# Convolution, norms and first queries of a streaming encoder step placed differently in the engines' queues

## What is computed

```python
def token_mixers(xn, hist_a, hist_b, w_in, ...):
    proj = xn @ w_in                                   # 2560 columns: h_a, c_a, b_a, v_b, g_b, 512 each
    conv_out_a, new_a = causal_dwconv(hist_a, c_a * h_a, conv_a_w)        # 3 taps
    y_a = rmsnorm(b_a * conv_out_a, out_norm_a_g)
    glu = v_b * sigmoid(g_b)
    conv_out_b, new_b = causal_dwconv(hist_b, glu, conv_b_w)              # 31 taps
    z = silu(layernorm(conv_out_b + conv_b_b, conv_norm_g, conv_norm_b))
    y_b = rmsnorm(z, out_norm_b_g)
    return concatenate([y_a, y_b]) @ w_out, new_a, new_b

h = x + token_mixers(rmsnorm(x), ...)
q = rmsnorm(h) @ w_q                                   # 2048 columns: 16 queries a token
x = h + peer(q, ...)                                   # top-k keys, 16384 single-neuron experts
y = rmsnorm(x)
```

## Time and profile before

| | us |
|---|---|
| median of 3 runs (1466.56 to 1467.59) | 1467.55 |
| the profiled execution | 1467.65 |
| span of its instructions | 1465.9 |
| before the first or behind the last of them | 1.75 |
| PE busy | 1448.5 (99%) |
| DVE busy | 1231.5 (84%) |
| POOL busy | 878.5 (60%) |
| ACT busy | 628.1 (43%) |
| mean granted TensorE clock | 0.995 |

### The profile page before, as it was taken

How to read it: one execution, slowest core, us unless ns; L and a number is a source line. 1 busy time by engine, 2 the same in 40 slices (tenths; PEclk the granted TensorE clock), 3 DMA queues, 4 the chain that set the end, 5 groups by cost and what they waited for, 6 DMA issues and landing times.

```text
span 1465.9 us, 25025 instructions
## 1 busy us (share of the span) xinstructions
PE 1448.5 (99%) x8592; PEld 1323.2 (90%) x8592; DVE 1231.5 (84%) x2517; ACT 628.1 (43%) x845; POOL 878.5 (60%) x551
## 2 busy tenths in 40 slices
PE   9998989999999999999999999999999999999998
PEld 9998989999999999999999999888888888888886
DVE  6998876898999999488788851799999999999995
ACT  6334543333333333467666754333333333333333
POOL 5686534556888888667666775255555555555510
PEclk9999999999999999999999999999999999999999
DMA  5321223567999999779999999899999999999962
GB/s 195 101 86 57 91 73 118 199 215 241 317 341 347 340 348 339 254 285 370 365 365 359 373 364 379 319 370 387 381 400 384 403 384 393 371 407 378 384 249 90
DMA packets 120259, 433.35 MB, mean 296 GB/s; under 512 B 12384, under 2 KB 12640, under 8 KB 118528
## 3 DMA queue, kind: packets, MB, share of 16 engines
q1 hardware_dynamic: 62592, 212.88, 40.3%
q0 software_dynamic: 46080, 167.79, 30.2%
q10 hardware_dynamic: 11520, 51.93, 8.9%
HBM read 379.34 MB, written 52.69 MB: 295 GB/s over the span
## 4 chain that ended last, share of the span: by engine, by line
PE 84%; DVE 1%; issue 0%; ACT 0%; DVEq 0%; ACTq 0%
PE ps_unit L861 36%; PE ps_misc L930 24%; PE ps_unit L930 12%; PE ps_unit L834 6%; PE ps_misc L896 3%; PE ps_misc L799 1%; PE ps_misc L803 0%; PE ps_unit L786 0%; PE ps_misc L926 0%; DVE gate L1577 0%; DVE gate_parts L1622 0%; PE ps_unit L926 0%; PE ps_misc L915 0%; PE ps_misc L817 0%; PE ps_misc L878 0%
## 5 line engine op out<-in xcount | busy, mean ns | idle before, releaser
L515 POOL TENSOR_TENSOR w_lo<-raw,w_hi 128x1024 fp32r<-128x1024 f32 x171 | 413.0, 2416 | 200.5 <-issue 120.9
L579 POOL DMA_INDIRECT rows<-v_rows,expert x160 | 256.7, 1604 | 243.0 <-DVE sums L1489 163.3
L976 ACT ACTIVATE w_hi<-raw 128x1024 fp32r<-128x1024 f32 x300 | 315.3, 1051 | 49.1 <-ACT act_ring L1152 31.8
L1196 ACT ACTIVATE prod_hi<-prod 128x384 fp32r<-128x384 f32 x128 | 67.3, 526 | 329.7 <-PE ps_unit L930 329.0
L861 PE MATMUL ps_unit<-mov_hi,w_hi 128*128 128x384 f32 x1024 | 204.6, 341 | 0.0
L861 PE MATMUL ps_unit<-mov_hi,w_lo 128*128 128x384 f32 x1024 | 199.9, 337 | 0.0
L861 PE MATMUL ps_unit<-mov_lo,w_hi 128*128 128x384 f32 x1024 | 199.9, 337 | 0.0
L1479 DVE CUSTOM_DVE_ANT_0 rows<-rows,ps_unit 128x1024 f32<-128x1024 f32 x160 | 189.5, 1213 | 5.5 <-DMA rows<-u_rows,expert 5.5
L861 PEld LDWEIGHTS ps_unit<-mov_lo,w_hi 128*128 128x128 f32 x1024 | 180.9, 188 | 0.0
L861 PEld LDWEIGHTS ps_unit<-mov_hi,w_lo 128*128 128x128 f32 x1024 | 180.9, 188 | 0.0
L861 PEld LDWEIGHTS ps_unit<-mov_hi,w_hi 128*128 128x128 f32 x1024 | 178.1, 188 | 0.2 <-issue 0.2
(11 more groups left out here) (263 smaller groups left out, 2563.0 us busy)
## 6 DMA issues: line engine op xcount, KB each, us to landing
raw<-stream SPq DMA_DIRECT2D x300, 512.0 KB, 6.1
acts_dram<-act_ring ACTq DMA_DIRECT2D x64, 384.0 KB
gates_dram<-gates ACTq DMA_DIRECT2D x12, 2048.0 KB, 10.9
acts_in<-acts_dram SPq DMA_DIRECT2D x32, 768.0 KB, 8.7
gates_even<-gates_dram SPq DMA_DIRECT2D x12, 1024.0 KB, 12.9
gates_odd<-gates_dram SPq DMA_DIRECT2D x12, 1024.0 KB, 13.2
rows<-u_rows,expert POOLq DMA_INDIRECT x160, 6.7
rows<-v_rows,expert POOLq DMA_INDIRECT x160, 8.4
```

The source lines that it names most:

```text
L515: nc.gpsimd.tensor_tensor(w_lo[:, j, :], raw[:, j, :], w_hi[:, j, :].bitcast(F32), ALU.subtract).then_inc(lo_made, 1)
L579: nc.gpsimd.indirect_dma_start(out=rows[:, n % ROWS_RING, :], out_offset=None, in_=table, in_offset=bass.IndirectOffsetOnAxis(ap=expert[:, ...
L976: nc.scalar.activation(w_hi[:, j, :], raw[:, j, :], ACT.Copy).then_inc(hi_made, 1)
L1196: nc.scalar.activation(prod_hi[:, v % RING], prod[:, v % 2], ACT.Copy).then_inc(prod_hi_made, 1)
```

## The change

The convolution's products: POOL makes `pad_b` for chunks 1 to 3 in its loop over units, at units 5, 7 and 9, ahead of that unit's wait for ACT. Chunk 0's stay on DVE, with the scaling of unit 1 that POOL had, and POOL waits for them. The sum of channels runs inside unit 19, between its second and third chunk. Of unit 20, the passes that need only `mov_hi` run as its chunks come, and the passes with `mov_lo` after the sum for the narrow norm. On DVE the last chunk's narrow taps are added before the `mov_low` steps, `reciprocal(2)` stands before the last of these, `reciprocal(3)` and the first two `add_output` come before the scaling of the layernorm, and the copies to the cache come after it. On ACT, the squares of the centred chunks precede the take of unit 19, the root's table is loaded at unit 8, and the squares of the narrow part follow `root(3)`. PE takes unit 23 before the sum for the second group's norm, runs 12 matmuls of ones by ones (`BUSY_FFN`) ahead of the queries, and takes the two first queries side by side, in the second half with a lag of three chunks. In unit 1, PE takes the second part of the first norm's sum of squares at k = 3 in place of 6. The diff's parts stand in the order POOL, PE, ACT, DVE.

```diff
                     split_low(0, 3)
                     pool.wait_ge(rstd_made, 1)
+                    pool.wait_ge(first_pad_made, 1)
...
+                if u in (5, 7, 9):
+                    n = (u - 3) // 2
+                    pool.wait_ge(sigmoid_made, n + 1)
+                    pool.wait_ge(in_scaled, 2 * n)
+                    pool.wait_ge(pads_ready, 1)
+                    times(pad_b[:, n, HIST_B:HIST_B + T_PROMPT], proj[:, 2 * n, 0:T_PROMPT],
+                          proj[:, 2 * n + 1, 0:T_PROMPT])
+                    times(pad_b[:, n, 2 * HIST_B + T_PROMPT:PAD_B], ...).then_inc(pad_b_made, 1)
...
+                    if c == WC - 1:
+                        step(times(b, b, rstd[:]))
+                        pool.wait_ge(taps_added, 1)
+                        times(h, h, b).then_inc(ya_made, 1)
+                        continue
...
                 for k in range(KC):
                     if k == 1:
                         square_sum(sq[:, KC - 1], sq_made, KC, False)
-                    if k == KC - 2:
+                    if k == 3:
                         square_sum(sq[:, 0], sq_added, 1, True)
...
-            with pe.Fori(1, N_IN // RING) as lap:
+            with pe.Fori(1, N_IN // RING - 1) as lap:
...
+            def sum_conv():
+                pe.wait_ge(conv_b_made, WC)
+                channel_sum(lambda c: proj[:, 2 * c], range(WC), WC, 0)
+
+            for j in range(RING):
+                pe.wait_ge(act_took, N_IN - RING + j - 1)
+                unit(N_IN // RING - 1, j, mov_hi, mov_lo, sum_conv if j == RING - 1 else None)
...
             channel_sum(lambda c: sq[:, c], range(WC), WC, 1, SQ_X + WC - 1)
+            pe.wait_ge(act_took, N_IN)
+            pe.wait_ge(hi_made, FIRST_OUT + 1)
+            pe.wait_ge(lo_made, FIRST_OUT + 1)
+            for k in range(WC):
+                pe.wait_ge(mov_hi_made, KC + k + 1)
+                for o in range(2):
+                    first_out(o, w_hi, mov_hi, k, first=(k == 0))
+                    first_out(o, w_lo, mov_hi, k)
             pe.wait_ge(a_added, 1)
             pe.wait_ge(sq_made, SQ_X + 2 * WC)
             channel_sum(lambda n: sq[:, (WC, KC - 1)[n]], range(2), 2, 0)
-            pe.wait_ge(act_took, N_IN)
-            out_unit(0, 0)
+            for o in range(2):
+                for k in range(WC):
+                    pe.wait_ge(mov_lo_made, KC + k + 1)
+                    ins = first_out(o, w_hi, mov_lo, k, last=(k == WC - 1))
+                ins.then_inc(unit_done if o else out_half_done, 1)
             out_unit(0, 1)
             out_unit(0, 2)
+            out_unit(0, 3)
             pe.wait_ge(dve_took, WC)
             pe.wait_ge(silu_added, 1)
             channel_sum(lambda c: sq[:, c], (0,), 1, 1)
-            out_unit(0, 3)
...
+                for a, lag in ((0, 0), (1, 3)):
+                    for k in range(KC + lag):
+                        for j, kj in ((0, k), (1, k - lag)):
+                            if not 0 <= kj < KC:
+                                continue
...
+            keep_busy(ps_unit[:, 0, 0:P], BUSY_FFN)
             first_queries()
...
+                if u == N_IN - 1:
+                    for n in range(WC):
+                        act.wait_ge(centred, n + 1)
+                        nc.scalar.activation(sq[:, n], proj[:, 2 * n], ACT.Square).then_inc(sq_made, 1)
                 if u > 0:
                     take(0, u, proj[:, u])
...
+            root(3, 1, 1.0 / WIDTH)
             act.wait_ge(ya_made, WC)
             group_high(WC - 1, ...)
             squares_a(WC - 1)
-            root(3, 1, 1.0 / WIDTH)
+            root(4, 0, 1.0 / WIDTH, out=std_a)
             split_high(first_out, 2)
             split_high(first_out, 3)
-            act.wait_ge(rstd_made, 2)
-            root(4, 0, 1.0 / WIDTH)
             act.wait_ge(cache_made, 1)
             act.dma_start(caches, cache_out[:]).then_inc(cache_saved, 16)
             for c in range(WC):
                 act.wait_ge(scaled_b, c + 1)
...
+            dve.wait_ge(sum_done, 2)
+            for c in range(WC):
+                nc.vector.scalar_tensor_tensor(out=halves(proj[:, 2 * c]), ...).then_inc(centred, 1)
+            dve.wait_ge(taps_made, WC)
...
+            nc.vector.tensor_tensor(h[:, 0:T_PROMPT], taps[0][:, 0:T_PROMPT], taps[2][:, 0:T_PROMPT],
+                                    ALU.add).then_inc(taps_added, 1)
+            for c in range(WC - 1):
+                mov_low(KC + c, c, proj[:, 2 * WC + 3 * c], par_col("out_a_g", c))
+            reciprocal(2, rstd_c)
             mov_low(KC + WC - 1, WC - 1, ...)
...
-            reciprocal(2, rstd[:])
-            dve.wait_ge(rstd_made, 2)
+            reciprocal(3, rstd_a, std_a)
+            dve.wait_ge(rstd_made, 3)
+            for q in range(2):
+                add_output(q, rstd_a)
             dve.wait_ge(centred, WC)
             for c in range(WC):
-                nc.vector.tensor_tensor(proj[:, 2 * c], proj[:, 2 * c], rstd[:], ALU.mult).then_inc(scaled_b, 1)
-            reciprocal(3, rstd_a)
-            dve.wait_ge(rstd_made, 3)
-            for q in range(KC - 2):
+                nc.vector.tensor_tensor(proj[:, 2 * c], proj[:, 2 * c], rstd_c, ALU.mult).then_inc(scaled_b, 1)
...
+            last.then_inc(cache_made, 1)
+            for q in range(2, KC - 2):
                 add_output(q, rstd_a)
             for c in range(WC):
                 mov_low(KC + WC + c, WC + c, proj[:, 2 * c + 1], par_col("out_b_g", c))
             for q in range(KC - 2, KC):
                 add_output(q, rstd_a)
```

More of the change, by code:

```diff
@@ L99 @@
 MADE_AHEAD = AHEAD + 1
+BUSY_FFN = 12
 WARM_UP = 12
@@ L285, in build @@
         a_added = sem("a_added")
+        taps_added = sem("taps_added")
         silu_added = sem("silu_added")
@@ L619, in _, with unit @@
         def _(pe):
-            def unit(lap, j, hi, lo):
+            def unit(lap, j, hi, lo, between=None):
                 u = RING * lap + j
@@ L626, in unit @@
                 for k in range(KC):
+                    if between and k == 2:
+                        between()
                     for n, (w, m) in enumerate(((w_hi, hi), (w_hi, lo), (w_lo, hi))):
@@ L632, in unit, with keep_busy @@
                 last.then_inc(unit_done, 1)
+            def keep_busy(out, times):
+                for n in range(times):
+                    nc.tensor.matmul(out, ones[:], ones[:], start=True, stop=True)
             def channel_sum(src, ks, chunks, to, n_sq=None):
@@ L734, in out_unit, with first_out @@
                     last.then_inc(unit_done if o else out_half_done, 1)
-            pe.wait_ge(conv_b_made, WC)
-            channel_sum(lambda c: proj[:, 2 * c], range(WC), WC, 0)
-            channel_sum(lambda c: sq[:, c], range(WC), WC, 1, SQ_X + WC - 1)
+            def first_out(o, w, mov, k, first=False, last=False):
+                at = (WC * o + k) * P
+                for a in range(2):
+                    ins = nc.tensor.matmul(out_psum(o)[:, a, :], w[:, 0, at:at + P], half(mov[:, k], a),
+                                           start=first, stop=last)
+                return ins
+            channel_sum(lambda c: sq[:, c], range(WC), WC, 1, SQ_X + WC - 1)
+            pe.wait_ge(act_took, N_IN)
[6 more added lines that the diff above has]
+                    first_out(o, w_lo, mov_hi, k)
             pe.wait_ge(a_added, 1)
@@ L771, in first_queries @@
             def first_queries():
[L773 to L778, removed]
+                for j in range(2):
+                    pe.wait_ge(hi_made, FIRST_Q + j + 1)
+                    pe.wait_ge(lo_made, FIRST_Q + j + 1)
+                for a, lag in ((0, 0), (1, 3)):
[3 more added lines that the diff above has]
+                                continue
                             if j == 0:
@@ L785, in first_queries @@
                             for m, (w, mov) in enumerate(((w_hi, mov_hi), (w_hi, mov_lo), (w_lo, mov_hi))):
[L786 to L790, removed]
+                                last = nc.tensor.matmul(unit_psum(j)[:, a, :], w[:, j, kj * P:(kj + 1) * P],
+                                                        half(mov[:, kj], a),
+                                                        start=(kj == 0 and m == 0), stop=(kj == KC - 1 and m == 2))
+                            if a == 1 and kj == KC - 1:
+                                last.then_inc(unit_done, 1)
             def head_scores(head, s):
@@ L981, in take, with root @@
                 nc.scalar.activation(halves(out), unit_psum(j % RING), func).then_inc(act_took, 1)
-            def root(n, to, scale):
+            def root(n, to, scale, out=std):
                 act.wait_ge(sum_done, n)
-                nc.scalar.activation(halves(std[:]), sum_psum(to), ACT.Sqrt, bias=eps[:], scale=scale).then_inc(std_made, 1)
+                nc.scalar.activation(halves(out[:]), sum_psum(to), ACT.Sqrt, bias=eps[:], scale=scale).then_inc(std_made, 1)
```

(6 more changed lines are left out.)

53 lines of the change are left out of this document (29 added, 24 removed).

## The result

| | before | changed |
|---|---|---|
| median of 12 runs each, us (lowest to highest) | 1467.30 (1465.06 to 1468.17) | 1470.43 (1469.58 to 1471.51) |
| ratio of the changed kernel to the one before | | 1.0022, 95% interval 1.0015 to 1.0030 |
| profiled execution: its time, its span | 1467.65, 1465.9 | 1470.34, 1468.5 |
| first queries end | 218.57 | 221.51 |
| from there to the end of the span | 1247.3 | 1247.0 |

The changed kernel is 3.1 us slower. The last two lines of the table carry the reading: what comes behind the first queries takes the same time in both to 0.3 us, so the whole loss lies before 221.51. Between the two profiled executions it is 2.7 us: the first queries end 2.9 us later, and the rest is 0.3 us shorter.

What follows compares the result with a forecast made beforehand. PE bounds from 220 us on, so the change is worth the shift of the first queries' end: +3.0 us by q = 10, +0.5 in the queries, +3.5 on 1467.65, giving 1471.0 for the median; range 1462.5 to 1473.5.

Steps and rivals of the forecast that it cites:

- a gain of 5 us up to the first output unit: PE ends unit 20 at 147.1, where the next unit began at 152.06 before: 4.9 us gained.
- silu's late start: ACT's queue holds silu behind the cache copies at 155.1; `silu_added` at 168.4, against about 162.3 before.
- the turns with POOL: DVE's `mov_low` and POOL's steps alternate by whole instructions; `mov_low` steps of 1.2 to 3.0 us in both groups.
- clock behind it, cost by q = 10: Half clock expected after PE's two waits around the second group's sum: 2.1 us, range 0 to 3.
- their net part: First queries: 1.2 us saved against 1.7 lost by a lowered clock; net +0.5, from -1.2 to +1.8.
- DVE gets through: Rival: `mov_low` pass between POOL's steps in both groups, q = 10 at 174.4, time 1463; chance 0.22.
- POOL keeps the lock: Rival: POOL holds the shared ports until its queue is empty, unit 24 starts 0.9 us later, 1472.5; chance 0.06.
- the clock holds: Rival: clock not lowered after PE's shortened waits, q = 10 at 179.7, queries save 1.2, 1467.7; chance 0.22.
- second fall: Lowered PE clock in the first queries' second half, behind a 1.5 us wait: 1.7 us, between nothing and 3.
- side by side: First queries: about 15 to 18 matmuls behind the last operand instead of 27, 1.2 us saved at full clock.
- the earlier root: Unit 1: first norm's second sum moves up three steps of 0.25 us; DVE could start 0.75 us earlier, left as margin.
- convolution late: Rival: the sum does not fit inside unit 19, a start 1.8 us late moves both chains, 1472.8; chance 0.06.

Runs made afterwards that it cites:

- the gated splits: POOL's split waits for the group's `mov_low`: unit 25's, against the changed kernel, 1468.06 us; unit 21's, added to the three moves without the lag, 1459.43 us.
- the first experiment: Against the changed kernel, ACT's wait for the cache copies and their transfer moved behind the split of unit 25; 1465.51 us, ratio 0.9989.
- the kernel with the three moves: Changed kernel with ACT's cache transfer and POOL's unit 25 split moved later, and `add_output(6)` between second-group `mov_low` two and three; 1462.29 us.
- the ones between the halves: Against the kernel with the three moves, 6 matmuls of ones in PE's wait between the first queries' two halves; 1461.40 us, ratio 0.9960.
- in turn: Against the kernel with the three moves, the two first queries in turn as before the change, the 12 ones kept; 1462.35 us, ratio 0.9967.
- the last kernel: Three moves without the lag, plus POOL's split of unit 21 waiting for the first group's first three `mov_low`; 1459.43 us, ratio 0.9947.

## Why the prediction was right

The forecast was 1471.0 us in 1462.5 to 1473.5, slower by 3.5; measured were 1470.43, slower by 3.1. The path was the forecast one: a gain of 5 us up to the first output unit, lost again through silu's late start, the turns with POOL and the clock. Its steps one by one, in the profile of the changed kernel:

| step | forecast | measured |
|---|---|---|
| unit 19 with the sum ends | 133.9 | 134.15, no wait behind it |
| fourth `mov_low` of the first group ends | 145.7 | 145.65 |
| PE's wait for it; next unit starts | 1.7; 147.1 | 1.14; 147.07 |
| ACT's cache transfer | 155.1 | 155.02 |
| `silu_added`; last `mov_low` ends | 168.4; 171.8 | 168.12; 171.48 |
| unit 24 starts | 173.3 | 173.09 |
| clock behind it, cost by q = 10 | 2.1 | 2.0 |
| q = 10 starts | 181.4 | 181.08 |
| first queries start | 205.5 | 205.29 |
| their net part | +0.5 | +0.2 |

- **The turns.** The order of the two engines was taken from one step of the trace before, 1.85 us instead of 0.70. It held for all seven steps, and the gated splits showed that the cause is the meeting: 7.93 became 5.83, 5.80 became 3.66. The rivals *DVE gets through* and *POOL keeps the lock* did not occur. The Trainium skill, page "SBUF — State Buffer", section "SBUF: two separate sides", says that between a DVE instruction with two SBUF inputs and a GpSimd one that reads SBUF, whichever begins first keeps the shared ports for the whole instruction and the other is fully blocked; the 0.6 us from the end of each POOL step to that of the `mov_low` behind it agree. That in each of these meetings the one that waited was next is what these runs add.
- **The clock.** The rival *the clock holds* was wrong for the kernel as changed, and right as a price: with the waits filled, 1.6 us came back. The prediction's ground for it, that waits of 3.86 and 2.83 us had both led to 0.50, was too simple. Behind 3.00 us in the first experiment the clock held, behind 1.41 us with pauses after it in the queries it fell. The kernels show that ones in the waits kept 1.00 here, and so did, in the queries, unbroken work behind the wait. They do not show a length of wait from which the clock falls, nor that PE's work alone sets the moment: with the same work up to the sum, it fell inside the second wait in the trace of the changed kernel, and at the sum with POOL's split moved. That stays open. So 2.1 forecast and 2.0 measured is in part luck: 2.1 was chosen between 0 and 3, and in the trace of the changed kernel without the lag, which is the same up to there, the stretch from unit 24 to the late halves took 20.72 us in place of 20.01.
- **The queries.** The second fall was forecast at 1.7 us. It came, and took about 1.3: in the kernel with the three moves, the queries end 3.71 us behind the last operand with it, 2.41 with the ones between the halves. That is the one term of the sum that was mis-sized, by 0.3. That the second fall needs the lag I had not seen: I priced side by side, lag included, at 1.2 us saved at full clock, which the ones between the halves bore out (2.41 against 3.61 in turn); without the lag 2.2 us were saved (1.40). The 8.8 us for 39 matmuls at half clock had no row beside it in the prediction; at half clock the changed kernel's trace has two matmuls in 0.45 us, which makes 8.8.
- **The convolution** was freer than I worked out. It ended at 122.1 (121.35 + 0.79), 7.5 us earlier than in the earlier trace rows, where 4.8 were counted: I left out the small product of each chunk (1.7 us, the group below) and took the earlier root as margin, which gave 0.5. I also did not count that the scaling of chunk 0 gets shorter: beside POOL it had taken 1.88 us, and now, with POOL waiting, 0.72. With chunk 0's products, which are shorter for the same reason, 3.9 of the 7.5 us are there before the first tap. The rival *convolution late* did not occur.
- **What I did not weigh enough.** The forecast has silu behind the cache's transfer in ACT's queue as one of many terms. Undone alone, it was worth 4.9 us, 1.6 of them by the clock: more than the whole loss. A chain forecast step by step gives a good time, but does not rank its own links; the undo did.

Chunk 0's scaling and the convolution's last step on DVE in the changed kernel, in order of time:

```profile
26.25 0.72 DVE L1411 TENSOR_TENSOR proj<-proj,rstd 128x544 f32<-128x544 f32 x1
...
121.35 0.79 DVE L1402 TENSOR_TENSOR proj<-proj,ps_misc 128x512 f32<-128x512 f32 x2
```

That scaling in the kernel before, in order of time:

```profile
26.10 1.88 DVE L1351 TENSOR_TENSOR proj<-proj,rstd 128x544 f32<-128x544 f32 x1
```

And the group that was left out, in the kernel before (busy us, mean ns of one):

```profile
L1358 DVE TENSOR_TENSOR pad_b<-proj 128x32 f32<-128x32 f32 x4 | 1.7, 418 | 0.0
```

## What to carry to other kernels

A gain on the critical engine is kept only if every other chain that meets it arrives earlier too: look for waits in a queue that the next operation does not need (here a cache transfer ahead of silu, worth 4.9 us with the clock that held once it was moved). Place elementwise steps of POOL where DVE runs instructions that are not blocked, such as the reciprocal, and let POOL wait for DVE's short steps rather than take turns with them. Filling one pause of PE can move the half clock to a place where it costs more; order the work behind a pause so that it does not break off again.

## What the hardware showed that I had not expected

- DVE's reciprocal took 3.54 us beside a POOL split of 2.39 us that ran in the same time (140.75 and 140.91 in the last kernel), while a `mov_low` beside a split took 2.86 to 2.91 in place of 0.68 to 0.78.
- Behind a wait of 2.69 us the next four matmuls ran at half clock in one execution (2.15 us), and at full clock in another (1.16 us), where the clock fell inside the next wait.
- Moving one transfer's issue and its wait in ACT's queue also moved the table load ahead, into idle time: 145.82 in place of 155.40.
